# A two-block transformer kernel on one core: first projection in three passes, 22 modulation sums moved, sparse values in one run

## The chip, the core and the metric

The kernel is one program on one core of a Trainium2 chip. Its engines are TensorE (PE in the profile, its weight loads PEld), VectorE (DVE), ScalarE (ACT), GpSimd (POOL) and SyncE (SP). SP and POOL issue the transfers. The metric is the device time of one execution in microseconds (us), lower is better; it is given as the median of several runs.

## What is computed

The input is a sequence of 512 tokens of width 1024, in float32. The first block has a mixer (window attention and a gated delta rule, both fed by one input projection), cross attention to 256 memory rows, and a SwiGLU feed-forward layer. The second block has four more feed-forward layers, a dilated attention and a sparse attention (compressed, selected and sliding branch); its norms are modulated by vectors made from a condition `c`. The parts that matter here:

```python
# first block: the input projection (w_in: 1024 x 2832)
h = _rms_norm(x, g_mix_pre[l])
proj = h @ w_in[l]
aq, ak, av, dqkv, dgate, dalpha, dbeta = jnp.split(proj, IN_SPLITS, axis=-1)
...
# its feed-forward layer
f = _swiglu(_rms_norm(x, g_ffn_pre[l]), w_gate_up[l], w_down[l])
```

The modulation is `silu(c) @ w_ada`, 160 x 128 numbers. Each group of 128 is one "modulation sum": 128 rows of 1024 weights, multiplied by `silu(c)` and summed along the row.

## The kernel before

The program is written engine by engine (`pe_run`, `act_run`, `dve_run`, and blocks for POOL and SP), with semaphores between them. What stands in those functions is the order in which an engine works; there is no scheduler. All activations are held with channels on the partitions: `h` is 8 tiles of 128 channels x 512 tokens. `e.stage_end(name)` is a meeting point of PE, ACT and DVE.

**Weights.** SP streams 128 x 4096 slabs into two slab buffers, in the order of `STREAM`; a buffer is loaded again when its last reader says so (`slab_used`). SP's queue is, in this order: vec (203 KB), const (194 KB), x in four transfers, slabs 0 and 1, `c_row`, positions, tables, then the slabs one by one.

**Two kinds of product.** In `pe_slab` and `pe_token_major` (rows of L735, L756 and L774) a matmul takes float32 operands straight from the slab. The trace records each such matmul as two instructions. In `pe_parts` and its kin (L794, L799 and L800) the weight and the activation are split in two parts of type float32r: `w_hi` (a rounded copy, made by ACT, `act_w_hi`, L1039), `w_lo` (the rest, a subtraction on DVE, `dve_w_lo`, L1216), `x_hi` and `x_lo` in the same way. A product is then three matmuls, hi x hi, lo x hi and hi x lo, each one instruction. There are four buffers (`PARTS`) for split weights, one slab quarter each. TensorE frees one when it has left it, ACT fills its `w_hi`, DVE its `w_lo`, so that the weights are up to four tiles ahead.

**The first projection** (stage `w_in`) has 22 feature tiles of 8 products and a token-major part (4 groups of tokens, 144 columns). Around it, DVE convolves the 12 tiles of the delta rule (L2912 and four times L2914) from what ACT copies out of the banks.

**The modulation sums** (`dve_ada`, L1450) are 160 DVE instructions, each on a 128 x 1024 row block that POOL loads (L3169, 512 KB each). They are put beside other work in three turns of `ADA_TURNS = (42, 35, 83)`: turn 0 in the first projection with five buffers, turn 2 in the first feed-forward layer with three. POOL loads the next block into a buffer when the sum on it is done.

**The feed-forward layer** runs in two halves of 12 and 10 hidden tiles. Each half has an expansion (for a pair of tiles, gate and up: product and split of one hidden tile, L1367 and L1370) and a down projection of 8 tiles. `modulations` says how many sums go where.

**Sparse attention** has 32 units of two heads and 128 queries, with b+1 key blocks, b from 0 to 3. For each unit, DVE takes the maximum (L2428), ACT the exponentials (L2460), DVE scales them (L2451, semaphore `weighed`), TensorE turns the weights (L2411, 6 to 18 blocks of 128 x 128, up to four to one of two banks), ACT copies each bank (L2471), and TensorE multiplies them by the values (L2394, 6 to 18 matmuls). The stages of three units overlap. In iteration i TensorE does the scores of unit i+1 (L2366), values of unit i-2, turns of unit i-1, with the values cut in shares that stand between the groups of turns.

## Time and profile before

| | us |
|---|---|
| median of three runs | 3896.53 (3895.29 to 3897.41) |
| profiled execution, device time | 3898.42 |
| its span in the profile | 3896.6 |
| first projection, from first product to last | 22.25 to 185.83 |
| sparse attention | 3269.80 to 3474.00 |

The page gives PE 94% of the span busy, DVE 48%, ACT 36%. A group of rows names line, engine, operation, the tiles written and read, then busy time and the mean of one. In brackets stands how long the engine was idle before, and what ended the wait.

### The profile page before, as it was taken

The page shows a single profiled execution, that of the slowest core. Times are in us where ns is not written, and L with a number is a line of the kernel's source. Part 1 is how long each engine was busy: PE and PEld are TensorE (multiplying, and loading weights), DVE is VectorE, ACT ScalarE, POOL GpSimd, SP SyncE. Part 2 cuts the span into 40 slices and gives each one's busy share as a digit, 9 for nine tenths or more (in the row PEclk, how much of TensorE's full clock was granted, in tenths as well). Part 3 has the DMA queues.
Part 4 walks back from the last instruction along what each step waited for, and adds up shares of the span by engine and source line. Part 5 has one row for each costly group of instructions (what it writes and reads, how often), then busy time and mean ns, then how long its engine had stood idle before and what let it go on. Part 6 is the DMA issues. An engine that isn't in the chain of part 4 may idle for free.

```text
span 3896.6 us, 49558 instructions
## 1 busy us (share of the span) xinstructions
PE 3678.8 (94%) x19120; PEld 2903.7 (75%) x19120; DVE 1886.0 (48%) x3841; ACT 1395.4 (36%) x2478; POOL 107.3 (3%) x183
## 2 busy tenths in 40 slices
PE   8879999989998999999999989999899998889999
PEld 3458975778887888776767768888788886568887
DVE  4656735566566333454555544333433345654333
ACT  1142212432233222455555543223322233763222
POOL 1100000011111000000000000000000000000000
PEclk9979999989999999999999989999999999999999
DMA  6500015426662232211111212222222221002222
GB/s 253 194 1 1 1 60 194 154 92 229 216 226 110 77 117 76 78 69 50 49 50 49 71 53 90 96 97 96 88 81 103 81 73 44 1 28 82 89 106 76
DMA packets 47157, 360.79 MB, mean 93 GB/s; under 512 B 5216, under 2 KB 5600, under 8 KB 28128
## 3 DMA queue, kind: packets, MB, share of 16 engines
q1 hardware_dynamic: 23472, 270.36, 18.9%
q0 software_dynamic: 23472, 87.50, 6.4%
q8 instruction: 144, 2.36, 0.3%
q14 instruction: 69, 0.57, 0.0%
HBM read 355.74 MB, written 2.10 MB: 92 GB/s over the span
## 4 chain that ended last, share of the span: by engine, by line
PE 85%; DVE 8%; issue 4%; ACT 2%; DVEq 1%; DMA 0%; PEld 0%; ACTq 0%; PEldq 0%; POOL 0%; SPq 0%; POOLq 0%
PE bank L794 20%; PE bank L800 20%; PE bank L799 20%; PE bank L756 5%; PE bank L1597 5%; PE bank L2411 2%; PE bank L1931 1%; PE bank L1948 1%; PE bank L2394 1%; PE bank L1919 1%; PE bank L774 1%; PE bank L1907 1%; PE bank L735 1%; PE bank L723 1%; PE bank L1894 1%
## 5 line engine op out<-in xcount | busy, mean ns | idle before, releaser
L794 PE MATMUL bank<-x_hi_sb,w_hi_sb 128*128 128x512 f32 x2712 | 1085.4, 400 | 54.8 <-DVE w_lo_sb L1216 15.4
L800 PE MATMUL bank<-x_hi_sb,w_lo_sb 128*128 128x512 f32 x2712 | 1064.0, 392 | 0.9 <-issue 0.9
L799 PE MATMUL bank<-x_lo_sb,w_hi_sb 128*128 128x512 f32 x2712 | 1063.1, 392 | 0.0
L794 PEld LDWEIGHTS bank<-x_hi_sb,w_hi_sb 128*128 128x128 f32 x2712 | 512.9, 189 | 196.7 <-issue 67.5
L1039 ACT ACTIVATE w_hi_sb<-slab_sb 128x1024 fp32r<-128x1024 f32 (+2 forms) x525 | 475.8, 930 | 438.0 <-PE bank L794 254.5
L1216 DVE TENSOR_TENSOR w_lo_sb<-slab_sb,w_hi_sb 128x1024 fp32r<-128x1024 f32 (+2 forms) x525 | 544.7, 1070 | 166.7 <-ACT w_hi_sb L1039 150.4
L800 PEld LDWEIGHTS bank<-x_hi_sb,w_lo_sb 128*128 128x128 f32 x2712 | 512.5, 189 | 113.1 <-issue 2.3
L799 PEld LDWEIGHTS bank<-x_lo_sb,w_hi_sb 128*128 128x128 f32 x2712 | 513.5, 189 | 100.8
L1367 DVE TENSOR_TENSOR hid_sb<-silu_gate_sb,bank 128x512 f32<-128x512 f32 x110 | 75.6, 688 | 620.4 <-PE bank L800 620.4
L794 PE MATMUL bank<-hid_hi_sb,w_hi_sb 128*128 128x512 f32 x880 | 343.3, 390 | 0.0
L800 PE MATMUL bank<-hid_hi_sb,w_lo_sb 128*128 128x512 f32 x880 | 342.8, 390 | 0.0
L799 PE MATMUL bank<-hid_lo_sb,w_hi_sb 128*128 128x512 f32 x880 | 342.8, 390 | 0.0
L1123 ACT ACTIVATE hid_hi_sb<-hid_sb 128x512 f32 (+1 forms) x110 | 69.5, 632 | 588.7 <-DVE hid_sb L1367 588.7
L800 PEld LDWEIGHTS bank<-hid_hi_sb,w_lo_sb 128*128 128x128 f32 x880 | 165.4, 188 | 34.5
L799 PEld LDWEIGHTS bank<-hid_lo_sb,w_hi_sb 128*128 128x128 f32 x880 | 165.5, 188 | 34.2
L794 PEld LDWEIGHTS bank<-hid_hi_sb,w_hi_sb 128*128 128x128 f32 x880 | 165.5, 188 | 34.2
L3020 DVE SCALAR_TENSOR_TENSOR h_sb<-bank,fold_sb,h_sb 128x512 f32<-128x512 f32 x64 | 48.1, 751 | 293.3 <-PE bank L800 293.3
L1120 ACT ACTIVATE silu_gate_sb<-bank 128x512 f32<-128x512 f32 x110 | 65.7, 597 | 265.8 <-PE bank L800 265.8
L1597 PE MATMUL bank<-sq_sb 128*128 128x128 f32 x1088 | 134.7, 288 | 6.3 <-DVE sq_sb L1790 6.3
L1597 PEld LDWEIGHTS bank<-sq_sb 128*128 128x128 f32 x1088 | 131.9, 203 | 9.4 <-DVE sq_sb L1790 7.4
L756 PE MATMUL bank<-xn_sb,slab_sb 128*128 128x512 f32 x288 | 124.8, 593 | 1.3 <-issue 1.3
L1450 DVE CUSTOM_DVE_ANT_0 keep_sb<-keep_sb,tables_sb 128x1024 f32<-128x1024 f32 x104 | 122.8, 1221 | 3.9 <-DMA keep_sb<-ada 2.7
(356 smaller groups left out, 3971.5 us busy)
## 6 DMA issues: line engine op xcount, KB each, us to landing
slab_sb<-weights SPq DMA_DIRECT2D x80, 2048.0 KB, 7.8
slab_sb<-weights SPq DMA_DIRECT2D x44, 1536.0 KB, 6.5
keep_sb<-ada POOLq DMA_DIRECT2D x104, 512.0 KB, 4.9
slab_sb<-weights SPq DMA_DIRECT2D x20, 1280.0 KB, 6.0
work_sb<-ada POOLq DMA_DIRECT2D x49, 512.0 KB, 5.4
tables_sb<-ada POOLq DMA_DIRECT2D x7, 512.0 KB, 6.5
h_sb<-x SPq DMA_DIRECT2D x4, 512.0 KB, 7.1
out<-h_sb SPq DMA_DIRECT2D x8, 256.0 KB, 2.0
```

Of the source, the lines that this page charges most:

```text
L756: mm = pe.matmul(bank[s][:, 0:width], slab[i][:, k * stride + t * P:k * stride + t * P + cols], x(k), start=k == 0, stop=k == nkt - 1)
L794: mm = pe.matmul(out, w_hi[p][:, w], hi, start=first, stop=False)
L799: pe.matmul(out, w_hi[p][:, w], lo, start=False, stop=False)
L800: return pe.matmul(out, w_lo[p][:, w], hi, start=False, stop=last)
L1039: e.eng.activation(w_hi[p][:, 0:cols], e.raw[:, quarter * cols:(quarter + 1) * cols], ACT.Copy).then_inc(w_hi_ready, 1)
L1120: act.activation(sg[:, :], bank[s][:, :], ACT.Silu).then_inc(gate_ready, 1)
L1123: act.activation(hid_hi[:, at + pair, :], hid[:, pair, :], ACT.Copy).then_inc(hid_hi_ready, 1)
L1216: dve.tensor_tensor(w_lo[p][:, 0:cols], slab[e.raw_at][:, quarter * cols:(quarter + 1) * cols], w_hi[p][:, 0:cols].bitcast(F32), ALU.subtr ...
L1367: dve.tensor_tensor(hid[:, pair, :], sg[:, :], bank[s][:, :], ALU.mult).then_inc(product_ready, 1)
L1450: dve.tensor_tensor_reduce(out=buf, in0=buf, in1=c_row, scale=1.0, scalar=0.0, op0=ALU.mult, op1=ALU.add, accum_out=mod[:, n:n + 1]).then_ ...
L1597: mm = pe.matmul(b[:, x * P:(x + 1) * P], l(x), r(x), start=n == 0, stop=n == len(prods) - 1)
L2411: mm = eng.transpose(turn_bank[t][:, (x - at) * P:(x - at + 1) * P], n_p[(i - 1) % 3][:, x * P:(x + 1) * P], ident)
```

## The change

The slabs of `w_in` are laid out tile by tile, and the projection uses split weights and a split activation (`dve_scale_split`), all in three passes. The token-major part gets 256 columns instead of 144. ACT splits the first slab before it takes the root of the norm. Of the 42 modulation sums in the projection 20 remain, on three buffers instead of five, and POOL loads their rows only when slab 0 has landed. The other 22 go to the first feed-forward layer: three per tile in the down projection of half 0, four instead of three per hidden tile in the expansion of half 1. In sparse attention all values of a unit stand in one run ahead of the wait for `weighed` and the turns. Places of buffers in `work` move with it.

```diff
-ADA_TURNS = (42, 35, 83)
+ADA_TURNS = (20, 35, 105)
...
+    ends = np.concatenate([*slabs_of(w_in[:, 20 * P:22 * P], P), *slabs_of(w_in[:, 22 * P:], 2 * P)], 1)
+    w_in = np.concatenate([slabs_by_tile(w_in[:, :20 * P]), ends[None]], 0)
...
-        ada_loaded = [[sem(f"ada_loaded{t}_{i}") for i in range(n)] for t, n in enumerate((5, 5, 3))]
-        ada_used = [[sem(f"ada_used{t}_{i}") for i in range(n)] for t, n in enumerate((5, 5, 3))]
+        ada_loaded = [[sem(f"ada_loaded{t}_{i}") for i in range(n)] for t, n in enumerate((3, 5, 3))]
+        ada_used = [[sem(f"ada_used{t}_{i}") for i in range(n)] for t, n in enumerate((3, 5, 3))]
...
-        b1_qkv = cut(work, 0, 12, S)
-        b1_vtm = cut(work, 6144, NB, 144)
-        b1_cv = [cut(work, 6720, S + 4), cut(work, 6720 + 516, S + 4)]
+        b1_qk = cut(work, 14336, 6, S)
+        b1_qkv = cut(work, 4096, 12, S)
+        b1_vtm = cut(work, 10240, NB, 144)
+        b1_cv = [cut(work, 10816, S + 4), cut(work, 10816 + 516, S + 4)]
         b1_gate = cut(keep, 0, 4, S)
-        b1_tmp = cut(work, 7760, 4, S)
+        b1_tmp = cut(work, 11848, 4, S)
         b1_cos, b1_sin = b1_tmp[:, 0, :], b1_tmp[:, 1, :]
 
-        P_SB = [cut(work, 9856 + 768 * i, 768) for i in range(3)]
-        PT = [cut(work, 12160 + 768 * i, 768) for i in range(2)]
+        P_SB = [cut(work, 11848 + 768 * i, 768) for i in range(3)]
+        PT = [cut(work, 14152 + 768 * i, 768) for i in range(2)]
...
+        def dve_scale_split(e, gain):
+
+            dve = e.eng
+            s = e.take(e.S, e.sc)
+            for i in range(KT + 2):
+                if i < KT:
+                    dve.scalar_tensor_tensor(out=y[:, i, :], in0=h[:, i, :], scalar=gain[:, i:i + 1],
+                                             in1=e.S.bank[s][:, :], op0=ALU.mult, op1=ALU.mult).then_inc(normed, 1)
+                if i >= 2:
+                    k = i - 2
+                    dve.wait_ge(x_hi_ready, e.nth(x_hi_ready))
+                    dve.tensor_tensor(x_lo[:, k, :], y[:, k, :], x_hi[:, k, :].bitcast(F32),
+                                      ALU.subtract).then_inc(x_lo_ready, 1)
+            dve.drain().then_inc(e.S.free[s], 1)
+
...
-        ada_bufs = [[cut(work, 9856 + D * i, D) for i in range(5)],
+        ada_bufs = [[cut(keep, 2048, D), cut(tables, 2688, D), cut(work, 11848, D)],
...
-                    groups = (blocks(units[i - 1][1]) + 3) // 4 if 1 <= i <= n else 0
-
-                    def values(share, shares):
-                        if i < 2:
-                            return
+                    if i >= 2:
                         tile, b = units[i - 2]
-                        kv, total = tile // 4, 1 + 2 * (b + 1)
-                        if share == 0:
-                            if i - 2 in opens:
-                                outs[tile] = e.give(e.A, e.acc)
-                            eng.wait_ge(copied, e.nth(copied))
-                        mm = None
-                        for x in range(total * share // shares, total * (share + 1) // shares):
+                        kv = tile // 4
+                        if i - 2 in opens:
+                            outs[tile] = e.give(e.A, e.acc)
+                        eng.wait_ge(copied, e.nth(copied))
+                        for x in range(1 + 2 * (b + 1)):
                             for hh in heads:
                                 br, k = (0, 0) if x == 0 else (1 + (x - 1) // (b + 1), (x - 1) % (b + 1))
                                 at = at_of(b, br, hh) + k * P
                                 v = n_vcmp[:, 64 * kv:64 * kv + 64] if br == 0 else \
                                     n_v[:, k, 128 * (br - 1) + 64 * kv:128 * (br - 1) + 64 * kv + 64]
                                 mm = eng.matmul(e.A.bank[outs[tile]][64 * hh:64 * hh + 64, b * P:(b + 1) * P], v,
-                                                n_pt[par][:, at:at + P], start=x == 0, stop=x == total - 1)
-                        if share == shares - 1:
-                            mm.then_inc(pv_done, 1)
-                            if i - 2 in closes:
-                                eng.drain().then_inc(e.A.full[outs[tile]], 1)
-
-                    shares = max(groups - 1, 1)
-                    values(0, shares)
+                                                n_pt[par][:, at:at + P], start=x == 0, stop=x == 2 * (b + 1))
+                        mm.then_inc(pv_done, 1)
+                        if i - 2 in closes:
+                            eng.drain().then_inc(e.A.full[outs[tile]], 1)
                     if 1 <= i <= n:
                         eng.wait_ge(weighed, e.nth(weighed))
                         total = blocks(units[i - 1][1])
                         for at in range(0, total, 4):
-                            if 2 <= at // 4 <= shares:
-                                values(at // 4 - 1, shares)
                             t = e.give(tp, e.tp)
                             for x in range(at, min(at + 4, total)):
                                 mm = eng.transpose(turn_bank[t][:, (x - at) * P:(x - at + 1) * P],
...
-            pe_slab_opening(e, xn, normed)
+            pe_parts_opening(e, x_hi, x_lo)
             for _ in range(4):
-                pe_slab(e, range(4), KT, 512, lambda k: xn[:, k, :])
-            pe_slab(e, range(2), KT, 512, lambda k: xn[:, k, :],
-                    more=[lambda sl: pe_token_major(e, sl, xn, KT, 256, 512, 144)])
+                pe_parts(e, PARTS, KT, x_hi, x_lo, by_tile=True)
+            e.slab.next()
+            for _ in range(2):
+                pe_tile_parts(e)
+            pe_token_parts(e, 2, 2 * P, 2 * P)
+            pe_settle(e)
+            e.seat(normed).pos += KT
...
+            for q in range(PARTS):
+                act_w_hi(e, q, D)
             act_sums_root(e, False)
+            for k in range(KT):
+                act.wait_ge(normed, e.nth(normed))
+                act.activation(x_hi[:, k, :], y[:, k, :], ACT.Copy).then_inc(x_hi_ready, 1)
             act.wait_ge(tables_first, 48)
             act.activation(c_row, c_row, ACT.Silu).then_inc(c_ready, 1)
             for t in range(22):
+                if t < 20:
+                    act_w_hi(e, t % PARTS, D)
                 if t < 4:
-                    act_copy(e, sq[:, t, :], scale=0.125)
+                    act_copy(e, b1_qk[:, t, :], scale=0.125)
                 elif t < 6:
-                    act_copy(e, sq[:, t, :])
+                    act_copy(e, b1_qk[:, t, :])
...
+            for q in range(PARTS):
+                dve_w_lo(e, q, D)
             dve_sums_done(e)
             e.sc.pos += 1
-            dve_scale(e, h, V("g_mix_pre"), xn, normed)
-            dve.wait_ge(c_ready, 1)
-            dve_ada(e, 14)
+            dve_scale_split(e, V("g_mix_pre"))
+            for t in range(6):
+                dve_w_lo(e, t % PARTS, D)
+                if t == 0:
+                    dve.wait_ge(c_ready, 1)
+                dve_ada(e, 2)
             e.acc.pos += 22
             for t in range(12):
+                dve_w_lo(e, (t + 6) % PARTS, D)
...
-                dve_ada(e, 1)
-            dve_ada(e, 16)
+            for q in (2, 3):
+                dve_w_lo(e, q, D)
+            dve_ada(e, 8)
...
                 if at in ("first", "mid", "last"):
-                    dve_ada(e, 3)
+                    dve_ada(e, 4 if half else 3)
                 elif half == 0 or at < 5:
-                    dve_ada(e, 2 if half == 0 and at < 4 else 1)
+                    dve_ada(e, 1 if half else 3)
...
-            eng.wait_ge(vec_loaded, 32)
+            eng.wait_ge(slab_loaded[0], 16)
```

`slabs_by_tile` is the layout that the feed-forward weights have already; in the expansion loop of `dve_ffn`, `modulations` is called once per hidden tile.

On DVE, at the start of the program, these are the rows before (L1229 adds squares, L1310 is the reciprocal of the RMS, L1317 scales the tiles, L1450 is a modulation sum in two instructions):

```order
L2892 MEMSET work_sb 128x2
L1229 TENSOR_TENSOR work_sb<-work_sb 128x512 x6
L1310 RECIPROCAL small_sb<-small_sb 128x4
L1317 SCALAR_TENSOR_TENSOR xn_sb<-h_sb,vec_sb,bank 128x512 x8
L1450 ISA work_sb,mod_sb<-work_sb,tables_sb 128x1024
L1450 ISA mod_sb 128x1
```

And these are they after (L1219 is now `w_lo`, L1313 the reciprocal, L1330 the scaling and L1335 `x_lo`):

```order
L1232 TENSOR_TENSOR work_sb<-work_sb 128x512 x6
L1219 TENSOR_TENSOR w_lo_sb<-slab_sb,w_hi_sb 128x1024 x4
L1313 RECIPROCAL small_sb<-small_sb 128x4
L1330 SCALAR_TENSOR_TENSOR y_sb<-h_sb,vec_sb,bank 128x512 x3
L1335 TENSOR_TENSOR x_lo_sb<-y_sb,x_hi_sb 128x512
L1330 SCALAR_TENSOR_TENSOR y_sb<-h_sb,vec_sb,bank 128x512
```

Four `w_lo` now stand ahead of the reciprocal, and three scalings ahead of the first `x_lo`.

On DVE, at the convolution tiles of the projection, before (L2912 and L2914 are one tile):

```order
L1450 ISA work_sb,mod_sb<-work_sb,tables_sb 128x1024
L1450 ISA mod_sb 128x1
L2912 TENSOR_SCALAR work_sb<-work_sb,vec_sb 128x512
L2914 SCALAR_TENSOR_TENSOR work_sb<-work_sb,vec_sb 128x512 x4
L1450 ISA work_sb,mod_sb<-work_sb,tables_sb 128x1024
```

and after (L1468 is the modulation sum, L2935 and L2937 are one tile):

```order
L1468 ISA work_sb,mod_sb<-work_sb,tables_sb 128x1024
L1468 ISA mod_sb 128x1
L1219 TENSOR_TENSOR w_lo_sb<-slab_sb,w_hi_sb 128x1024
L2935 TENSOR_SCALAR work_sb<-work_sb,vec_sb 128x512
L2937 SCALAR_TENSOR_TENSOR work_sb<-work_sb,vec_sb 128x512 x4
L1219 TENSOR_TENSOR w_lo_sb<-slab_sb,w_hi_sb 128x1024
```

The sum behind each convolution tile is gone, and a `w_lo` stands ahead of each.

On TensorE, in sparse attention, one iteration before (scores of the next unit, values of a unit with b = 1, turns of a unit with b = 2, the 31-column scores):

```order
L2366 MATMUL bank<-keep_sb,work_sb 128x256 x4
L2394 MATMUL bank<-work_sb,keep_sb 64x128 x2
L2411 MATMUL bank<-const_sb,work_sb 128x128 x8
L2394 MATMUL bank<-work_sb,keep_sb 64x128 x4
L2411 MATMUL bank<-const_sb,work_sb 128x128 x4
L2394 MATMUL bank<-work_sb,keep_sb 64x128 x4
L2411 MATMUL bank<-const_sb,work_sb 128x128 x2
L2366 MATMUL bank<-keep_sb,work_sb 128x31 x2
```

and the same iteration after, with the start of the next (L2384 scores, L2406 values, L2417 turns):

```order
L2384 MATMUL bank<-keep_sb,work_sb 128x256 x4
L2406 MATMUL bank<-work_sb,keep_sb 64x128 x10
L2417 MATMUL bank<-const_sb,work_sb 128x128 x14
L2384 MATMUL bank<-keep_sb,work_sb 128x31 x2
L2384 MATMUL bank<-keep_sb,work_sb 128x512 x4
```

Eight of the ten value matmuls have moved ahead of the first turn, where TensorE waits for `weighed`, and the fourteen turns follow each other.

## Rows read from the trace of the kernel before

**Rows 1.** The page: the chain that ended last, by engine
```profile
PE 85%; DVE 8%; issue 4%; ACT 2%; DVEq 1%; DMA 0%; PEld 0%; ACTq 0%; PEldq 0%; POOL 0%; SPq 0%; POOLq 0%
```

**Rows 2.** Windows: stretch, length, busy PE, PEld, DVE, ACT, POOL, clock, DMA, GB/s
```profile
22.25:185.83 163.58, 162.24 (x416) 75.12 (x416) 97.03 (x154) 14.21 (x23) 19.53 (x37) 1.00 0.55 206
...
3269.80:3474.00 204.20, 169.47 (x1536) 113.59 (x1536) 134.33 (x709) 153.72 (x507) 0.00 (x0) 0.95 0.01 1
```

**Rows 3.** Timelines of DVE and POOL, landings of L3169: first layer, half 1
```profile
1060.21 0.69 DVE L1367 TENSOR_TENSOR hid_sb<-silu_gate_sb,bank 128x512 f32<-128x512 f32 x1 [3.00 <-PE bank L800]
...
1062.31 1.22 DVE L1450 CUSTOM_DVE_ANT_0 keep_sb<-keep_sb,tables_sb 128x1024 f32<-128x1024 f32 x1
...
1065.75 2.36 DVE L1216 TENSOR_TENSOR w_lo_sb<-slab_sb,w_hi_sb 128x1024 fp32r<-128x1024 f32 x2
1071.09 0.69 DVE L1367 TENSOR_TENSOR hid_sb<-silu_gate_sb,bank 128x512 f32<-128x512 f32 x1 [2.98 <-PE bank L800]
...
1063.83 0.53 POOL L3169 DMA_DIRECT2D keep_sb<-ada  x1 [8.07 <-DVE mod_sb L1450]
...
DMA to landing us min/median/max: 3.3/4.8/5.4
```

**Rows 4.** Timeline of PE: one slab of the first projection
```profile
80.10 27.70 PE L756 MATMUL bank<-xn_sb,slab_sb 128*128 128x512 f32 x64 [0.26 <-issue]
```

**Rows 5.** Line L873: third pass of a token-major part, durations and starts
```profile
L873 PE MATMUL bank<-w_lo_sb,x_hi_sb x32: 277/283/415, 2770.3 to 2783.0; 128*128 128x256 f32 x32
```

**Rows 6.** Timeline of PE: second and third matmul of the first layer
```profile
835.28 0.63 PE L799 MATMUL bank<-x_lo_sb,w_hi_sb 128*128 128x512 f32 x1
835.71 0.63 PE L800 MATMUL bank<-x_hi_sb,w_lo_sb 128*128 128x512 f32 x1
```

**Rows 7.** Timeline of DVE and PE: start of the projection
```profile
19.01 0.18 DVE L1310 RECIPROCAL small_sb<-small_sb 128x4 f32<-128x4 f32 x1 [4.03 <-ACT small_sb L992]
...
21.35 5.36 DVE L1317 SCALAR_TENSOR_TENSOR xn_sb<-h_sb,vec_sb,bank 128x512 f32<-128x512 f32 x8 [2.17 <-PE bank L966]
...
22.25 29.62 PE L735 MATMUL bank<-xn_sb,slab_sb 128*128 128x512 f32 x64 [0.93 <-DVE xn_sb L1317]
```

**Rows 8.** DMA, 0 to 40 us (GB/s: slices of 1 us), and landings of L3218
```profile
GB/s 0 29 286 190 266 356 311 320 422 418 397 406 467 397 434 426 434 426 438 406 426 422 418 377 414 391 425 422 475 376 409 108 0 0 0 0 66 311 295 262
...
slab_sb<-weights SPq DMA_DIRECT2D x2, 2048.0 KB, 18.9
h_sb<-x SPq DMA_DIRECT2D x4, 512.0 KB, 7.1
...
3.56 1.25 SPq L3218 DMA_DIRECT2D slab_sb<-weights  x2
...
DMA to landing us min/median/max: 16.1/18.9/21.7
```

**Rows 9.** Timelines of DVE and ACT: a convolution tile, two w_hi
```profile
101.60 0.49 DVE L2912 TENSOR_SCALAR work_sb<-work_sb,vec_sb 128x512 f32<-128x512 f32 x1 [2.08 <-ACT work_sb L2715]
...
105.16 1.22 DVE L1450 CUSTOM_DVE_ANT_0 work_sb<-work_sb,tables_sb 128x1024 f32<-128x1024 f32 x1
...
1061.58 1.99 ACT L1039 ACTIVATE w_hi_sb<-slab_sb 128x1024 fp32r<-128x1024 f32 x2
```

**Rows 10.** Timeline: one iteration of sparse attention (L2366 is the next scores)
```profile
3394.75 1.09 PE L2411 MATMUL bank<-const_sb,work_sb 128*128 128x128 f32 x8 [1.33 <-DVE work_sb L2451]
...
3395.52 1.07 ACT L2471 ACTIVATE sq_sb<-bank 128x512 f32<-128x512 f32 x2
3395.78 0.66 PE L2394 MATMUL bank<-work_sb,keep_sb 128*64 128x128 f32 x8
3396.36 0.66 PE L2411 MATMUL bank<-const_sb,work_sb 128*128 128x128 f32 x4
...
3397.91 2.21 PE L2366 MATMUL bank<-keep_sb,work_sb 64*128 64x31 f32 x12
```

**Rows 11.** Waits in sparse attention: who waited for whom, us, times, longest
```profile
PE bank L2411 <- DVE work_sb L2451: 18.3, 16, 3.7
```

12 lines of the change are left out of this document (6 added, 6 removed).

## Prediction

> **What bounds the kernel now.** I began with the page. TensorE is on the chain that ended last for 85% of the span, DVE for 8% [rows 1]. So a stage gets shorter if TensorE has less to do there, or if a wait in front of it goes. The change touches three stages, and I read each by its stretch, then by its timeline. In the first projection TensorE is busy 162.24 us of 163.58 while DVE has 97.03 of work [rows 2]: TensorE bound, others with room. In sparse attention it is busy 169.47 of 204.20 us, with ACT at 153.72 and DVE at 134.33 [rows 2]; there the three engines wait for each other. In the first feed-forward layer I read the timeline instead: DVE does its work for a pair of tiles and then waits 2.98 us for TensorE [rows 3], so TensorE sets the pace and DVE has that much room.
>
> **Projection, TensorE's work.** A product is one 128x128 weight tile times 512 tokens. As float32 it is recorded as two instructions, and a slab of 32 products takes 27.70 us, 0.865 us each [rows 4]. The same product in three passes of the split form stands in the feed-forward layer: one pair of tiles, 16 products, from 1060.21 to 1071.09, is 10.88 us, so 0.680 us [rows 3]. Before the change the stage has 22 tiles of 8 products plus the token-major part. After it, 176 x 0.680 = 119.7 us. The token-major part becomes 96 matmuls of 256 columns. The same shape runs elsewhere, with 32 triplets whose starts span 12.7 us over 31 steps [rows 5], so 13.1 us. After an idle stretch the first matmuls come every 0.43 us [rows 6] instead of 0.227 (10.88 / 48), the lower clock of 1.2 GHz against 2.4. Nine of them cost 1.8 us more. With 0.6 us for drains the stage is 135.2 us of TensorE time where it was 163.58: 28.4 saved.
>
> **Projection, its start.** Before, the first product starts at 22.25, right after the first scaled tile [rows 7]. Now it needs the slab split too, and the order shows the four w_lo subtractions ahead of the reciprocal of the RMS. So the start is: slab 0 landed, w_hi of the first quarter on ACT (about 1.05 us), four w_lo on DVE, then reciprocal, spread, three scales, one x_lo. Slab 0 lands at 3.6 + 16.1 = 19.7 us now [rows 8]. Ahead of it in its queue are vec and const (0.4 MB) and x (four times 512 KB); with its own 2048 KB that is 4.6 MB [rows 8]. The 1 us slices of moved bytes add up to 4.6 MB at 14.8 us [rows 8], and the five modulation rows that share those slices now will wait for slab 0. Bounds: 14.8 if nothing else is moved and the last byte counts, 19.7 as before. I take 16.0. Then 16.0 + 1.05 + 4 x 1.15 (two w_lo take 2.36, [rows 3]) = 21.7. From reciprocal to first scale it is 2.34 us, from 19.01 to 21.35 [rows 7]. Three scales at 0.67 (5.36 for eight, [rows 7]) and one subtraction of 512 columns, about 0.7, give 26.7. That is 4.5 us later than 22.25 (3.3 to 8.2 by the bounds).
> From 10 to 30 us the slices show 377 to 475 GB/s [rows 8]. The Trainium skill (DMA: Bandwidth & Descriptors, Where 436 GB/s comes from) says that for HBM to SBUF the HBM side binds, near 358 GB/s. By that rate, as an estimate, slab 0 would land about 1 us later than I take; the trace of this core, alone on its memory, is above it, so the trace decides.
>
> **Projection, do ACT and DVE keep up?** A tile is 8 x 0.680 = 5.44 us of TensorE. A convolution tile costs DVE 3.56 us (101.60 to 105.16, [rows 9]); with a w_lo of 1.15 that is 4.7, and the sum of 1.15 that stood there is gone, or it would be 5.9. The first six tiles carry w_lo and two sums: 3.5 us. ACT has a w_hi (two take 1.99, [rows 9]) and a copy of 512 columns. Weights are made four tiles ahead, so a late one is absorbed. At the end the last w_lo can be done about 21 us before TensorE is (two gate tiles and the token-major part follow it), and eight sums over three buffers need some 15 (three rounds of 1.15 + 0.4 + 3.6). All this is hidden; if w_hi, w_lo, copy and convolution stood in series instead, some 6.3 us per tile, twelve tiles would give back 10 us. Net of the stage: 28.4 - 4.5 = **23.9 us saved**.
>
> **The 22 sums in the feed-forward layer.** In half 0 the down projection goes from two or one to three sums per tile; a tile lasts 12 x 0.680 = 8.16 us there, and DVE then has three sums (3.4), two w_lo of 768 columns (about 1.8) and one copy (under 1). Hidden. In half 1 each pair gets a fourth sum, but there are three buffers. Now a group starts at 1062.31; the first sum's buffer is asked for again at 1063.83, and a row lands 3.3 to 5.4 us after its issue, median 4.8 [rows 3]. The first of a group has the queue to itself, so I take 3.6 for it. The fourth sum then starts not 3.44 but about 5.2 us after the group's start (4.9 to 6.4 by the minimum and the median), ends at 6.3, and two w_lo end at 8.6. DVE's next product is due 8.78 after the group's start (1071.09), and 2.98 of them are idle now [rows 3]. So 2.9 us are added to a slack of 2.98. What is late next is the w_lo: its first is needed by TensorE at the end of the running pair, 1.3 us after it is made. Beside slab loads the group runs up to 0.9 us over. Over ten pairs I take **1.0 us lost**, bounds 0 and 9 (0.9 each). If the cover were gone, each sum would cost 1.15 us, 11.5 for the ten.
>
> **Sparse attention.** Each unit of TensorE is: scores ahead, values of the unit before the last, a wait for DVE's weights, then turns in groups of four through two banks. Now most of the values stand between the turns. Counted over a round of 16 units, 88 of 192 value matmuls stand behind the wait, in two rounds 176. Four, recorded as eight, take 0.58 us (3395.78 to 3396.36, [rows 10]), so 0.117 x 176 = 20.5 us move ahead of the wait. TensorE waits there for weights in two of their three buffers alone 18.3 us in 16 waits, 1.14 us each [rows 11]; 12 units of 16 have something to move, 0.86 us on average. The cover is uneven, since a heavy unit meets a short wait; I take three quarters, 15.5 us. Then the turns have nothing between them and meet ACT. In the unit at 3394.75, eight turns are out after 1.03 us, but ACT starts copying them only at 3395.52, 0.54 us each [rows 10]. The third group can start at 3395.52 + 0.54 + 0.06 = 3396.12, 0.35 after the first eight, and the block ends at 2.33 us instead of 3.16 (3397.91, [rows 10]). The wait in front, 1.33, takes the moved 0.93 us. So this unit gains 0.83. The copy's pace costs 0.35 to 0.45 in each of the 24 units, some 8.5 in all. Net **7.0 us saved**; the ends are 0 (turns fully paced by ACT, or the loop over DVE and ACT as long as now) and 15.5 (no pacing).
>
> **The sum.** 23.9 - 1.0 + 7.0 = 29.9. The profiled execution took 3898.42 us with a span of 3896.6; its own time would be 3868.5. It lies 1.9 us above the median of the three runs, 3896.53, against which I set the forecast: 3866.6.
>
> **The rivals.**
> *A, the turns are ACT's.* ACT is busy 153.72 of 204.20 us [rows 2] and every copy stands behind its exponentials. If the loop exponentials, copies, turns, scores sets the unit, the run of values brings nothing: 3873.6. Against it: in the unit I followed ACT idles between copies. Chance 0.12.
> *B, DVE becomes the pace of half 1.* For it: 0.1 us of slack left per pair, and a median landing of 4.8 us [rows 3]. With 0.9 per pair: 3874.6. Chance 0.10.
> *C, a late start.* Slab 0 lands as before, or the w_hi are paced otherwise: 3.7 us more, 3870. Chance 0.08.
> *D, DVE paces the projection's convolution tiles*, 6.3 us a tile: 10 given back, 3876.6. Against: four tiles of lead. Chance 0.05. Should it wait for the last sums at the stage's end as well, another 15 us is lost and the time is within 0.2% of now; 0.02.
> *E, slower.* One mechanism: in half 1 the fourth sum holds the w_lo so long that TensorE idles each pair and falls to the lower clock, where a matmul takes 0.43 instead of 0.227 us [rows 6]. 48 matmuls a pair are then 9.7 us longer, ten pairs 97: 3963. It decides from 3.9 us lost per pair on (39 in all, against the 31 of the other two terms); the fourth sum would have to start 9 us after the group's start, where the longest landing here gives 7.0. Chance 0.03.
> My forecast, with small shifts of its terms, has the remaining 0.60.
>
> **How the numbers follow.** The low end is the projection with slab 0 at 14.8 (1.2 more), no loss in the layer, and sparse attention near 14.4: 3857. The high end takes in A, B, C and D alone and A with B: 3882. Outside lie some 15 in 100. This kernel's measurement tells about 0.2%, 7.8 us, from no change. Faster by more: 0.95; within: 0.02; slower: 0.03.
>
> **What would show it.** In the changed profile: first three-pass product near 26.7; 5.44 us per tile, no wait for w_lo after the first four; last token-major matmul near 162; slab 0 landed near 16; in half 1 a wait of DVE for the modulation row of 1 to 2.5 us before each fourth sum, pairs still 10.88 to 11.1; in the sparse stage the wait for DVE down from 18.3 to under 9 us, a new wait of turns for ACT of some 9. Wrong would be: tiles of over 5.6 us, TensorE's wait for w_lo in half 1 above a microsecond a pair, or a sparse stage still above 200 us.

## Result, and the profile after

The changed kernel takes 3867.02 us (median, 3863.18 to 3869.01) against 3896.54: ratio 0.9925, 95% interval 0.9912 to 0.9938, 29.5 us less. The forecast was 3866.6. It was right in the sum and wrong in two of its three terms, which cancelled:

| | forecast, us | in the profile | the edit by itself on the chip |
|---|---|---|---|
| projection | 23.9 saved | 24.7 saved | 22.1 saved (beside a fourth row buffer; by the interval of the ratio 14 to 25) |
| 22 sums in the feed-forward layer | 1.0 lost | 12.1 lost | 12.3 lost |
| sparse attention | 7.0 saved | 16.9 saved | 16.3 saved |
| together | 29.9 | 29.5 | |

The profiled execution is the fastest of its four (3863.18, span 3861.4); its span is 35.2 under the one of before. That the three terms read from the profiles add up to the same 29.5 as the two medians is chance. The 5.7 us beyond the three terms lie in stages that the change does not touch, 4.5 of them between the first down tile of the second feed-forward layer and sparse attention. In the profiles of this study, with the same code there, that stretch varied from 1896 to 1906 us.

The page of the changed kernel, the chain by engine and two groups:

```profile
PE 83%; DVE 8%; issue 4%; ACT 3%; DVEq 1%; DMA 1%; PEld 0%; ACTq 0%; PEldq 0%; POOL 0%; SPq 0%; POOLq 0%
...
L797 PE MATMUL bank<-x_hi_sb,w_hi_sb 128*128 128x512 f32 x2888 | 1156.7, 401 | 61.6 <-DVE w_lo_sb L1219 19.3
...
L1468 DVE CUSTOM_DVE_ANT_0 keep_sb<-keep_sb,tables_sb 128x1024 f32<-128x1024 f32 x133 | 157.9, 1220 | 44.6 <-DMA keep_sb<-ada 42.7
```

TensorE is still the chain (before 85%, [rows 1]). What is new is in the other rows: TensorE waits more for `w_lo`, and DVE 42.7 us for modulation rows, where before it was 2.7.

**The projection.** The start, a timeline of all engines, and the landing of the first two slabs:

```profile
16.17 3.90 ACT L1042 ACTIVATE w_hi_sb<-slab_sb 128x1024 fp32r<-128x1024 f32 x4 [3.56 <-DMA slab_sb<-weights]
...
17.25 4.63 DVE L1219 TENSOR_TENSOR w_lo_sb<-slab_sb,w_hi_sb 128x1024 fp32r<-128x1024 f32 x4 [4.53 <-ACT w_hi_sb L1042]
...
22.02 0.18 DVE L1313 RECIPROCAL small_sb<-small_sb 128x4 f32<-128x4 f32 x1
...
24.37 2.06 DVE L1330 SCALAR_TENSOR_TENSOR y_sb<-h_sb,vec_sb,bank 128x512 f32<-128x512 f32 x3 [2.17 <-PE bank L969]
...
27.18 0.77 PE L797 MATMUL bank<-x_hi_sb,w_hi_sb 128*128 128x512 f32 x1 [2.85 <-DVE x_lo_sb L1335]
```

```profile
DMA to landing us min/median/max: 12.6/14.7/16.9
```

The slab lands at 3.56 + 12.6 = 16.2 and DVE splits from 17.25 on; then reciprocal, spread, scales, and the first product at 27.18, 4.9 later than [rows 7]. The windows of three stretches (columns as in [rows 2]): the projection, the expansion of half 1, sparse attention. Below them, from the timeline, the first matmul of the next stage, which started at 197.10 before:

```profile
27.18:160.98 133.80, 132.91 (x624) 111.66 (x624) 95.87 (x135) 37.98 (x49) 8.96 (x17) 1.00 0.45 165
1022.46:1128.86 106.40, 101.44 (x433) 83.00 (x432) 73.91 (x109) 27.52 (x36) 19.01 (x36) 0.97 0.73 253
3252.20:3439.84 187.64, 158.52 (x1536) 112.38 (x1537) 134.12 (x709) 152.36 (x507) 0.00 (x0) 0.97 0.01 2
```

```profile
172.41 7.63 PE L791 MATMUL bank<-work_sb,const_sb 128*128 128x512 f32 x12 [11.27 <-ACTq L497]
```

The projection is 133.8 us at a granted clock of 1.00 where it was 163.58 [rows 2]; only its first seven matmuls came every 0.43 us, although that row gives them the same clock. In the waits of this stretch TensorE has none for `w_lo`. DVE waited 17.0 us for rows, and TensorE did not wait for it.

**Half 1 of the feed-forward layer.** Its ten products take 106.40 us from first to last; nine steps of 10.88 would be 97.9. From the last down tile of half 0 (1011.58) to the last of half 1 it is 180.7 us, before 168.6. Waits of 1000 to 1195, and the fourth sum of a usual group, of a late one and of the last one (timeline of DVE):

```profile
DVE keep_sb L1468 <- DMA keep_sb<-ada: 23.5, 11, 5.3
...
PE bank L797 <- DVE w_lo_sb L1219: 7.5, 3, 3.3
```

```profile
1029.68 1.22 DVE L1468 CUSTOM_DVE_ANT_0 keep_sb<-keep_sb,tables_sb 128x1024 f32<-128x1024 f32 x1 [1.62 <-DMA keep_sb<-ada]
...
1079.75 1.23 DVE L1468 CUSTOM_DVE_ANT_0 keep_sb<-keep_sb,tables_sb 128x1024 f32<-128x1024 f32 x1 [5.33 <-DMA keep_sb<-ada]
...
1136.06 1.23 DVE L1468 CUSTOM_DVE_ANT_0 keep_sb<-keep_sb,tables_sb 128x1024 f32<-128x1024 f32 x1 [1.69 <-DMA keep_sb<-ada]
```

The landing of the row that each of two groups waited for, by its issue:

```profile
L3193 POOL DMA_DIRECT2D keep_sb<-ada x1: 528/528/528, 1037.0 to 1037.0; - x1
...
DMA to landing us min/median/max: 3.5/3.5/3.5
```

```profile
L3193 POOL DMA_DIRECT2D keep_sb<-ada x1: 527/527/527, 1072.4 to 1072.4; - x1
...
DMA to landing us min/median/max: 7.3/7.3/7.3
```

And what SP had issued ahead of the second, and what TensorE did then (timelines):

```profile
1068.68 0.34 SPq L3232 DMA_DIRECT2D slab_sb<-weights  x1
```

```profile
1082.17 0.80 PE L797 MATMUL bank<-x_hi_sb,w_hi_sb 128*128 128x512 f32 x1 [3.33 <-DVE w_lo_sb L1219]
1082.77 0.63 PE L802 MATMUL bank<-x_lo_sb,w_hi_sb 128*128 128x512 f32 x1
1083.19 0.63 PE L803 MATMUL bank<-x_hi_sb,w_lo_sb 128*128 128x512 f32 x1
...
1138.18 0.47 PE L797 MATMUL bank<-hid_hi_sb,w_hi_sb 128*128 128x512 f32 x1 [2.56 <-DVE w_lo_sb L1219]
```

In a usual group the first buffer's row lands after 3.5 us and the fourth sum waits 1.6: what the forecast said, and the pair keeps its 10.88. Eight of the ten groups are like this, with landings of 3.5 to 3.7 us. The two others asked for the row 3.6 and 3.8 us after SP had issued a 2 MB slab load. There the row needs 6.4 or 7.3 us, the `w_lo` is late, and TensorE stands for 1.6 and 3.3 us. (A row asked for 6.9 us after such a load landed in 3.6 us, so it depends on how far the load is.) The third wait, 2.6 us, is another case. Its row landed in the usual 3.7 us, but it is the last group, and the `w_lo` behind its fourth sum is the one that the down projection needs.

After the gap of 3.33 a matmul comes every 0.43 us instead of 0.227: the granted clock of 1082.17 to 1087.90 is 0.50, 1.2 GHz against 2.4. Fourteen matmuls then take 2.9 us too long. Behind the third wait the granted clock of 1139.40 to 1144.00 is 0.63, and nine matmuls take 1.6 us too long. Behind the first, of 1.64 us, it stays 1.00. 7.5 us of waits and 4.5 us of lower clock are 12.0 of the 12.1. The Trainium skill (DMA: Bandwidth & Descriptors, Queues, rings and completion order) says that a DMA engine goes round robin between the queues it has work for; by that rule a row on POOL's queue shares each engine with a slab on SP's, and the trace agrees, with 3.5 against 6.4 and 7.3 us.

**Sparse attention.** It is 187.6 us long where it was 204.5. TensorE's waits ahead of turns, and one iteration, the one of [rows 10]:

```profile
PE bank L2417 <- DVE work_sb L2457: 8.0, 10, 2.6
...
PE bank L2417 <- ACT sq_sb L2477: 5.3, 14, 1.0
PE bank L2417 <- ACT work_sb L2477: 5.0, 16, 0.6
...
PE bank L2417 <- DVE xn_sb L2457: 2.8, 3, 1.0
```

```profile
3365.80 1.31 PE L2406 MATMUL bank<-work_sb,keep_sb 128*64 128x128 f32 x20
3367.57 1.09 PE L2417 MATMUL bank<-const_sb,work_sb 128*128 128x128 f32 x8 [0.46 <-DVE work_sb L2457]
3368.97 0.93 PE L2417 MATMUL bank<-const_sb,work_sb 128*128 128x128 f32 x6 [0.31 <-ACT sq_sb L2477]
3369.83 2.21 PE L2384 MATMUL bank<-keep_sb,work_sb 64*128 64x31 f32 x12
```

Waits for DVE are down to 10.8 us (with the third buffer 24.3 before), waits for ACT in front of turns up from nothing to 10.3, each new group 0.31 in this unit: near the forecast. The waits in front of turns that the profile puts down to "issue" went from 5.8 to 0.8 us besides. This unit takes 2.26 us from first turn to next scores, where the forecast said 2.33.

The forecast had left out two things. One is in the run lengths. A run is a row of matmuls of one kind with none of the other between them: 8 turns take 1.03 us and 4 take 0.59 [rows 10], which is 0.11 each and 0.15 for the run. Going through the shares of all units, 96 such runs are gone. The other is the clock. Below are windows of the kernel before and of that of experiment 4 (`thin_shares`): the whole stage of each, then a stretch at the lower clock of each (in these, only TensorE's busy time, clock and DMA):

```profile
3269.85:3474.34 204.49, 169.47 (x1536) 113.56 (x1536) 134.33 (x709) 153.96 (x507) 0.00 (x0) 0.95 0.01 1
...
3253.40:3455.86 202.46, 172.01 (x1537) 115.47 (x1537) 134.16 (x709) 154.18 (x507) 0.00 (x0) 0.93 0.01 1
...
3381.50:3384.50 3.00, 3.00 (x17) 0.50 0.02 5
...
3407.50:3414.00 6.50, 6.38 (x34) 0.50 0.00 0
```

(The row of the changed kernel is the third of the windows above.) TensorE's idle time in the stage went from 35.0 to 29.1 us and its busy time from 169.5 to 158.5, together the 16.9. Counted in windows of 0.5 us, TensorE was busy for 17 us of the stage at a granted clock of 0.50 before and for 7 us after. At half speed that is 8.6 and 3.7 us lost, so 4.9 of the 11.0 us of busy time are the clock. In the profiles of this study the loss is 7.3 to 8.7 us with the order of before and 2.2 to 6.9 with the new one. So it goes with the order, but it varies, and it is not the price of the runs.

### The profile page after: what moved, and what is told of

It reads as the page before. It is cut to its first block, busy times and chain, and to the rows that moved or that the text cites. A ratio compares the mean times of both kernels' runs of the same rounds, so it can differ in the third digit from the quotient of the medians.

```text
span 3861.4 us, 50061 instructions
## 1 busy us (share of the span) xinstructions
PE 3639.3 (94%) x19328; PEld 2940.1 (76%) x19328; DVE 1916.9 (50%) x3873; ACT 1421.8 (37%) x2510; POOL 107.3 (3%) x183
## 4 chain that ended last, share of the span: by engine, by line
PE 83%; DVE 8%; issue 4%; ACT 3%; DVEq 1%; DMA 1%; PEld 0%; ACTq 0%; PEldq 0%; POOL 0%; SPq 0%; POOLq 0%
PE bank L797 21%; PE bank L802 21%; PE bank L803 21%; PE bank L1615 5%; PE bank L759 2%; PE bank L1949 1%; PE bank L1937 1%; PE bank L1966 1%; PE bank L2417 1%; DVE w_lo_sb L1219 1%; PE bank L2384 1%; PE bank L1925 1%; PE bank L777 1%; PE bank L726 1%; PE bank L2406 1%
## 5 line engine op out<-in xcount | busy, mean ns | idle before, releaser
L797 PE MATMUL bank<-x_hi_sb,w_hi_sb 128*128 128x512 f32 x2888 | 1156.7, 401 | 61.6 <-DVE w_lo_sb L1219 19.3
L803 PE MATMUL bank<-x_hi_sb,w_lo_sb 128*128 128x512 f32 x2888 | 1134.0, 393 | 0.0
L802 PE MATMUL bank<-x_lo_sb,w_hi_sb 128*128 128x512 f32 x2888 | 1133.9, 393 | 0.0
L797 PEld LDWEIGHTS bank<-x_hi_sb,w_hi_sb 128*128 128x128 f32 x2888 | 547.4, 190 | 211.9 <-issue 71.2
L1042 ACT ACTIVATE w_hi_sb<-slab_sb 128x1024 fp32r<-128x1024 f32 (+2 forms) x549 | 500.9, 936 | 508.3 <-PE bank L797 319.6
L1219 DVE TENSOR_TENSOR w_lo_sb<-slab_sb,w_hi_sb 128x1024 fp32r<-128x1024 f32 (+2 forms) x549 | 573.4, 1076 | 185.2 <-ACT w_hi_sb L1042 168.7
L803 PEld LDWEIGHTS bank<-x_hi_sb,w_lo_sb 128*128 128x128 f32 x2888 | 546.9, 189 | 117.7
L802 PEld LDWEIGHTS bank<-x_lo_sb,w_hi_sb 128*128 128x128 f32 x2888 | 548.1, 190 | 107.8
L1468 DVE CUSTOM_DVE_ANT_0 keep_sb<-keep_sb,tables_sb 128x1024 f32<-128x1024 f32 x133 | 157.9, 1220 | 44.6 <-DMA keep_sb<-ada 42.7
L1388 DVE TENSOR_TENSOR hid_lo_sb<-hid_sb,hid_hi_sb 128x512 f32 (+1 forms) x110 | 76.1, 692 | 93.8 <-ACT hid_hi_sb L1126 93.8
```

The lines of the kernel that those rows point to most:

```text
L797: mm = pe.matmul(out, w_hi[p][:, w], hi, start=first, stop=False)
L802: pe.matmul(out, w_hi[p][:, w], lo, start=False, stop=False)
L803: return pe.matmul(out, w_lo[p][:, w], hi, start=False, stop=last)
L1042: e.eng.activation(w_hi[p][:, 0:cols], e.raw[:, quarter * cols:(quarter + 1) * cols], ACT.Copy).then_inc(w_hi_ready, 1)
L1219: dve.tensor_tensor(w_lo[p][:, 0:cols], slab[e.raw_at][:, quarter * cols:(quarter + 1) * cols], w_hi[p][:, 0:cols].bitcast(F32), ALU.subtr ...
L1388: dve.tensor_tensor(hid_lo[:, at + pair, :], hid[:, pair, :], hid_hi[:, at + pair, :].bitcast(F32), ALU.subtract).then_inc(hid_lo_ready, 1)
```

## Experiments

Each was timed beside the kernel before, which gave 3895.4 to 3897.6. The changed kernel gave 3867.02 at first and 3864.78 in experiment 9, so a difference to it is uncertain by some 2 us.

**1. Sparse attention alone.** The kernel before with the block of the change on sparse attention, nothing else.

> The kernel before with only the sparse values in one run. The changed kernel's sparse stage took 187.6 us where it took 204.5, 16.9 less. Theory T1 (the gain belongs to this edit: 13.5 us less waiting for DVE, 96 fewer changes between value and turn matmuls at about 0.15 us each, less some 10 us of new waits for ACT): 3896.5 - 17 = 3879.5, range 3876 to 3883. Rival R1, the prediction's 7.0 (the rest came from the run or from elsewhere): 3889.5. Rival R2, nothing: 3896.5.

3879.2 us, ratio 0.9959 (0.9945 to 0.9972): 16.3 saved, and the stage is 187.1 us long. The gain belongs to this edit; the prediction's 7.0 is too small by more than half. What T1 gives as its parts this run does not separate.

**2. The 22 sums alone**, on the kernel before.

```diff
-ADA_TURNS = (42, 35, 83)
+ADA_TURNS = (20, 35, 105)
...
-            dve_ada(e, 14)
+            dve_ada(e, 12)
...
-                dve_ada(e, 1)
-            dve_ada(e, 16)
+            dve_ada(e, 8)
...
-                    dve_ada(e, 3)
+                    dve_ada(e, 4 if half else 3)
                 elif half == 0 or at < 5:
-                    dve_ada(e, 2 if half == 0 and at < 4 else 1)
+                    dve_ada(e, 1 if half else 3)
```

> The kernel before with only the 22 modulation sums moved to the first feed-forward layer; the projection stays in float32 with five row buffers. Theory T2 (the fourth row of a group in half 1 lands too late beside the slab loads, TensorE waits for w_lo three times and runs at the lower clock after it): 12 to 14 us slower, 3909.5. Where the slab loads fall against the groups may shift with the projection, so 6 to 16. Rival R3, the prediction's 1.0: 3897.5. Rival R4 (in the projection DVE's 42 sums had cost TensorE something, which comes back): below 3896.5.

3907.77 us, ratio 1.0032 (1.0020 to 1.0045): 12.3 lost, 11.8 of it between the last down tiles of the two halves. The waits of half 1 are there without the new projection:

```profile
DVE keep_sb L1450 <- DMA keep_sb<-ada: 24.4, 11, 5.2
...
PE bank L794 <- DVE w_lo_sb L1216: 7.2, 3, 3.1
```

**3. A fourth row buffer in half 1.** The changed kernel; the buffer takes the place of hidden tiles 10 and 11, which half 1 has not.

```diff
-                    [cut(keep, D * i, D) for i in range(3)]]
+                    [*(cut(keep, D * i, D) for i in range(3)), cut(work, 9216, D)]]
...
                 if n < pieces:
+                    if turn == 2:
+                        if n < 60:
+                            i, use = n % 3, n // 3
+                        else:
+                            i = (n - 60) % 4
+                            use = (n - 60) // 4 + (20 if i < 3 else 0)
+                        return ada_bufs[2][i], ada_loaded[2][i], ada_used[2][i], use
```

> The changed kernel with a fourth row buffer for the sums of half 1 (in the place of two hidden tiles that half 1 does not use); the same sums at the same places. Theory T2 (it is the reload of the first buffer, not DVE's own work): all four rows of a group are asked for a pair ahead, the pairs are back at 10.88 us, 11 to 13 us gained: 3867 - 12 = 3855. Rival R5 (DVE's four sums and two w_lo alone are too long, or the DMA engines cannot carry four rows a pair beside the slabs): no more than 3 us gained, 3864.

3853.15 us, ratio 0.9892 (0.9877 to 0.9907), 13.9 under the changed kernel (11.6 under its second median). TensorE's waits for `w_lo` in this stretch, and a group on DVE with its four sums in a row:

```profile
PE bank L797 <- DVE w_lo_sb L1219: 0.8, 1, 0.8
```

```profile
1057.27 0.69 DVE L1385 TENSOR_TENSOR hid_sb<-silu_gate_sb,bank 128x512 f32<-128x512 f32 x1 [1.84 <-PE bank L803]
...
1062.80 1.22 DVE L1475 CUSTOM_DVE_ANT_0 work_sb<-work_sb,tables_sb 128x1024 f32<-128x1024 f32 x1
...
1068.15 0.69 DVE L1385 TENSOR_TENSOR hid_sb<-silu_gate_sb,bank 128x512 f32<-128x512 f32 x1 [1.85 <-PE bank L803]
```

Same sums, same places, same bytes; only the reload is no longer waited for. The pairs are back at 10.88, and DVE has 1.85 us left in each. From the last down tile of half 0 to that of half 1 it is 170.6 us, against 180.7 and, before the change, 168.6. So 10.1 of the 12.1 us were the wait for the row and what came of it. The other 2.0 stay with four sums per group, 0.8 of them as the wait above, at the down projection. R5 falls for the most part: neither DVE's own work nor the DMA engines' total was too much within the pairs.

**4. One pair of values between the turns.** The changed kernel in sparse attention with the shares of before, but so cut:

```diff
-                        for x in range(total * share // shares, total * (share + 1) // shares):
+                        lead = total - shares + 1
+                        for x in (range(lead) if share == 0 else range(lead + share - 1, lead + share)):
```

> The changed kernel, but in sparse attention each share behind the first keeps one pair of value matmuls between the groups of turns (48 of them, 96 changes of kind more than in the changed kernel); all other values stay ahead of the wait. Theory T1 (a change costs about 0.15 us, so 96 are 14.4, and what they fill is about 10 us of waits for ACT): slower than the changed kernel by 2 to 7 us, 3871. The prediction's own account (no price for a change, the turns' wait for ACT 8.5 us, filled by 48 pairs of 0.22 us): faster by 4 to 8 us, 3861.

3879.77 us, ratio 0.9957 (0.9943 to 0.9971), 12.8 over the changed kernel (15.0 over its second median). The prediction's account has the wrong sign. T1 has the right one, but I had the size too small. Waits, and a piece of one iteration:

```profile
PE bank L2430 <- DVE work_sb L2470: 13.9, 13, 3.7
...
PE bank L2430 <- DVE xn_sb L2470: 3.8, 4, 2.0
...
PE bank L2430 <- ACT sq_sb L2490: 1.2, 2, 0.6
```

```profile
3376.90 0.44 PE L2413 MATMUL bank<-work_sb,keep_sb 128*64 128x128 f32 x4
3377.28 0.66 PE L2430 MATMUL bank<-const_sb,work_sb 128*128 128x128 f32 x4
3377.87 0.44 PE L2413 MATMUL bank<-work_sb,keep_sb 128*64 128x128 f32 x4
```

The waits of turns for ACT are gone but for 1.6 us, as both said. Four turns take 0.59 us (3377.28 to 3377.87), four recorded values 0.38. The stage is 14.8 us longer than the changed kernel's, by the windows above: 13.5 more busy for the same matmuls and 1.3 more idle. In the idle time, 8.7 us less for ACT met 6.9 more for DVE and 5.0 more under "issue". In the busy time, 8.1 us are the lower clock (24 us busy at 0.50 instead of 7, half of it lost), which neither theory had; only this one profile shows this order. The 5.4 left are less than 96 x 0.15 = 14.4. A sum of waits cannot settle this, since the end of a run in front of a wait is counted as busy (eight turns as 1.09 us, 1.03 without a wait behind them). So the 0.15 us per change is shown in single rows, and its share of the stage's gain is not.

Against the kernel before, the stage is only 2.0 us shorter. There 80 of the 176 value matmuls have moved ahead of the wait, and the number of runs is the same. So moving values brought little here as long as the runs stayed; 3.2 us more of lower clock than before are in that figure.

**5. Is it the tile shape?** The kernel before, its values with 128 columns. It leaves out attention's right values, and only its times count.

```diff
-                                v = n_vcmp[:, 64 * kv:64 * kv + 64] if br == 0 else \
-                                    n_v[:, k, 128 * (br - 1) + 64 * kv:128 * (br - 1) + 64 * kv + 64]
-                                mm = eng.matmul(e.A.bank[outs[tile]][64 * hh:64 * hh + 64, b * P:(b + 1) * P], v,
-                                                n_pt[par][:, at:at + P], start=x == 0, stop=x == total - 1)
+                                v = n_vcmp[:, 0:P] if br == 0 else n_v[:, k, 128 * (br - 1):128 * br]
+                                mm = eng.matmul(e.A.bank[outs[tile]][:, b * P:(b + 1) * P], v,
+                                                n_pt[par][:, at:at + P], start=x == 0 and hh == 0,
+                                                stop=x == total - 1 and hh == 1)
```

> The kernel before, sparse values in shares, but each value matmul takes 128 value columns instead of 64 and writes the whole bank, so that both heads add up in one place (the values are no longer attention's; the number, order, rows and waits of the matmuls are the same). A value matmul is then a 128*128 tile as a turn is, and not 128*64. In the trace a run of n recorded matmuls of either kind takes 0.15 us + n x 0.055 (values) or n x 0.11 (turns): 4 values 0.37, 2 turns 0.37. Theory T3 (the 0.15 us is the price of going from one tile shape of TensorE to another): runs of 4 values between turns take 0.22 instead of 0.37, 128 changes between values and turns cost nothing, up to 19 us less TensorE time, of which waits take some back: 3884, range 3878 to 3889. Rival T4 (the 0.15 us is a price of every change of operands or banks, whatever the shape): 3896.5, runs of 4 still 0.37.

3918.03 us, ratio 1.0050 (1.0038 to 1.0062), 22.6 slower: neither theory's time. The timeline says why, and still decides between them:

```profile
3407.94 1.06 PE L2393 MATMUL bank<-work_sb,keep_sb 128*128 128x128 f32 x8
3408.84 0.60 PE L2411 MATMUL bank<-const_sb,work_sb 128*128 128x128 f32 x4
3409.27 1.06 PE L2393 MATMUL bank<-work_sb,keep_sb 128*128 128x128 f32 x8
```

Four turns between two runs of values now take 0.43 us (3408.84 to 3409.27) where they took 0.59: the 0.15 is gone once both kinds have one tile shape. T3 holds for these runs, T4 falls. But eight recorded value matmuls take 0.90 instead of 0.58, 0.11 each instead of 0.055. Over 768 that is some 44 us. The two heads' matmuls go to the two 64-column halves in turn. They may have run side by side, or a matmul of 64 columns may take half the time by itself; all of them in this kernel alternate between the halves, so no run here tells the two apart. The Trainium skill (TensorEngine Tiling (Array Packing), Key Properties) says that a change of tiling mode drains the engine, and that tiles work independently. The trace fits both, at 0.15 us for a change of shape.

**6. Rows asked for early.** The changed kernel with one line as it was:

```diff
-            eng.wait_ge(slab_loaded[0], 16)
+            eng.wait_ge(vec_loaded, 32)
             load_ada(0)
```

> The changed kernel, but POOL asks for the first three modulation rows when vec has landed, as in the kernel before, and not when slab 0 has. The step of the prediction: slab 0 landed at 19.7 with five rows beside it and at 16.2 with none; three rows are 1.5 MB, at some 420 GB/s 3.7 us. So slab 0 near 19, the first product near 30 instead of 27.18, the time 3869.5 (2 to 3.5 us over the changed kernel's 3867.0). Rival: the rows only take bandwidth that the slab does not need: first product within 1 us of 27.2.

3865.93 us, ratio 0.9917 (0.9903 to 0.9930). In the profile slab 0 lands at 3.6 + 17.6 = 21.2, and the first product is at

```profile
32.22 0.76 PE L797 MATMUL bank<-x_hi_sb,w_hi_sb 128*128 128x512 f32 x1 [2.85 <-DVE x_lo_sb L1335]
```

5.0 later, more than the 3.7 that I had from the bytes. In the kernel before, five rows asked for just as early left slab 0 at 19.7 [rows 8], 3.5 later than 16.2. So the delay is real, but its size does not follow from the number of rows. The next stage starts 5.4 later too, and the first down tile of the second feed-forward layer still 5.6; by the end of the profile 2.4 are left. The median is 1.1 below the changed kernel's (1.1 above its second one), and the intervals of the two ratios allow some -10 to +4 us. So the late start is shown by the profile, and that it costs its 5 us at the end is not: whether they are won back behind the layer or lost in the scatter of the stages there stays open.

**7. Root and reciprocal ahead of the split weights.** The changed kernel; in DVE's order `dve_sums_done(e)` goes ahead of the four `dve_w_lo` in the same way.

```diff
+            act_sums_root(e, False)
             for q in range(PARTS):
                 act_w_hi(e, q, D)
-            act_sums_root(e, False)
```

> The changed kernel with two orders swapped at the start: ACT takes the root of the norm ahead of the four w_hi, DVE the reciprocal ahead of the four w_lo. The reciprocal then falls in DVE's idle time before slab 0 (near 17 instead of 22.02) and its 2.34 us of spreading lie under the w_lo. First product near 24.8 instead of 27.18, 2.4 us gained: 3864.6. If instead something else holds the start (the slab, or x_hi), less than 1 us.

3862.41 us (3855.47 to 3865.95), ratio 0.9906 (0.9892 to 0.9919); first product at 26.33, 0.85 earlier instead of 2.4. The median is 2.4 under the changed kernel's second one, but its own runs lie 10 apart, so what the start brings can't be read from it. ACT's timeline shows what is late now, the root that the `w_hi` wait for:

```profile
17.21 0.26 ACT L995 ACTIVATE small_sb<-bank,small_sb 128x4 f32<-128x4 f32 x1 [3.85 <-PE bank L959]
17.65 3.90 ACT L1042 ACTIVATE w_hi_sb<-slab_sb 128x1024 fp32r<-128x1024 f32 x4 [0.17 <-issue]
```

**8. Root and reciprocal behind the first split weight, with the fourth buffer.**

```diff
-            for q in range(PARTS):
-                act_w_hi(e, q, D)
+            act_w_hi(e, 0, D)
             act_sums_root(e, False)
+            for q in range(1, PARTS):
+                act_w_hi(e, q, D)
...
-            for q in range(PARTS):
-                dve_w_lo(e, q, D)
+            dve_w_lo(e, 0, D)
             dve_sums_done(e)
             e.sc.pos += 1
+            for q in range(1, PARTS):
+                dve_w_lo(e, q, D)
```

> The changed kernel with the fourth row buffer and, at the start, ACT: first w_hi, root, three w_hi; DVE: first w_lo, reciprocal, three w_lo. With the root ahead of all w_hi the first w_hi waited for it until 17.65 although slab 0 was there a microsecond earlier, and the first product came at 26.33 and 26.61. Now the root waits behind one w_hi and ends near 17.7, the reciprocal stands behind the first w_lo, near 18.6, its spreading ends near 21, under the other w_lo. First product 25.2 (against 27.2 to 27.6 in the changed order), 2 us gained: 3851.2. If the reciprocal comes too late for that, 26.3 as with the root first.

3852.18 us, ratio 0.9889 (0.9874 to 0.9904); timeline of the start:

```profile
22.48 2.07 DVE L1330 SCALAR_TENSOR_TENSOR y_sb<-h_sb,vec_sb,bank 128x512 f32<-128x512 f32 x3 [0.15 <-issue]
...
25.29 0.77 PE L797 MATMUL bank<-x_hi_sb,w_hi_sb 128*128 128x512 f32 x1 [4.35 <-DVE x_lo_sb L1335]
```

First product at 25.29, as expected, 1.9 us earlier. That is the fastest kernel of the study, 43.4 us under the kernel before and 12.6 under the changed kernel's second median. The fourth buffer has nearly all of it (3853.15 without the start); 1.9 us are too little to see in the median.

**9. Combinations and a control.** The edits of 3 and 7 together:

> The changed kernel with the fourth row buffer and with root and reciprocal first. Both are at different places and should add up: 3853.2 - 2.4 = 3850.8. If the earlier start shifts slab loads against the row groups of half 1, up to 2 us either way.

3853.47 us, ratio 0.9883 (0.9868 to 0.9898), first product at 26.61: the start's part is too small to see beside 3853.15.

Eleven sums moved on from half 1 instead of a fourth buffer, on the changed kernel:

```diff
-ADA_TURNS = (20, 35, 105)
+ADA_TURNS = (20, 46, 94)
...
-            dve_ada(e, 8)
+            dve_ada(e, 14)
             dve_sums_done(e)
...
-            dve_linear_parts(e, y, 2, lambda k: dve_ada(e, 3 if k < 3 else 2))
+            dve_linear_parts(e, y, 2, lambda k: dve_ada(e, 3))
...
-                    dve_ada(e, 4 if half else 3)
-                elif half == 0 or at < 5:
+                    dve_ada(e, 3)
+                elif half == 0 or at < 4:
```

> The changed kernel with 11 of the modulation sums moved on from half 1 of the first feed-forward layer: six to DVE's idle time of 13 us before the cross attention, five to its query projection. Half 1 is back at three sums per pair and four buffers are not needed. Theory T2: as the fourth buffer, 11 to 13 us gained, 3855; should the sums of the query projection come late for their w_lo, up to 3 us are given back. Rival R5 (four sums and two w_lo of DVE as such were not the cause, the later rows of turn 1 delay TensorE elsewhere): 3862 or more.

3856.82, ratio 0.9888 (0.9873 to 0.9903). Half 1 has no wait for `w_lo`, and from last down tile to last down tile it is 168.7 us, as before the change, which confirms T2 by another way. Some of it is lost again ahead of it, where the sums went: from the first matmul behind the projection to the first down tile it is 787.2 us, in the changed kernel 782.1 (in the other profiles up to 784.9).

The projection alone, as the kernel of experiment 3 with the sparse attention of before:

> The kernel with the fourth row buffer (3853.15 us) and the sparse attention of before, values in shares: what the projection in three passes brings when the two other parts are taken out. Theory: the parts add up, 3853.2 + 16.3 (what one run of values gave alone) = 3869.5, that is 27 us under the kernel before, the 24.7 by which the last product of the stage is earlier, and 1 to 3 in other stages. Rival: the parts help each other and the sum of the single ones is off by more than 5 us.

3873.4 (3868.94 to 3879.83), ratio 0.9949 (0.9936 to 0.9963): 22.1 saved, 4 less than the sum of the parts says and within its scatter; the next stage starts at 172.91, 0.5 later than in the changed kernel.

And the changed kernel once more:

> The changed kernel once more, unaltered, beside the two others of this call, as a measure of how far its median moves: 3867.0, within 2 us. Its profile should again show three waits of TensorE for w_lo in half 1, if they come from the phase of the slab loads and not from chance: the stage then loses 12 to 14 us again.

3864.78, ratio 0.9923 (0.9910 to 0.9937), with TensorE's three waits for `w_lo` in half 1 again (7.9 us). They are no chance of one run.

## Why the prediction was right, and where it was not

**Projection.** Right step by step. TensorE's part is 133.8 (135.2 forecast), a product 0.680, seven slow matmuls instead of nine. The token-major part took 11.6 us where the forecast had 13.1. The 0.6 us for drains in the sum is in no run. Slab 0 landed at 16.2 (16.0), the first product came at 27.18 (26.7), the last token-major matmul at 160.87 (162). ACT and DVE kept up, so rival D did not happen. Rival C neither, though experiment 6 shows that its cause, rows ahead of the slab, is real.

**Sums.** The mechanism was right and the size was not. The step that failed is "The first of a group has the queue to itself, so I take 3.6 for it". It had POOL's queue to itself, not the DMA engines: in two groups of ten, early in a slab load, the landing is 6.4 and 7.3. Besides, the forecast counted pairs only, and the last group's `w_lo` is for the down projection, where TensorE stood 2.6 us at a landing of 3.7. The clock behind the waits, 4.5 us, was priced in rival E alone. The bound of 9 took only the 5.4 of the kernel before, where three sums on three buffers never asked for the row at once. The range of the term was 0 to 9; it measured 12. Rival B named the wait and "0.9 per pair"; in truth seven groups of ten lose nothing and three lose 2 to 6 us, in part as lower clock. Rival E's chain (late `w_lo`, idle TensorE, lower clock) happened in small: for six and for three microseconds, not for the stage.

**Sparse attention.** Cover and pacing were near: 13.5 us less waiting for DVE, 18.5 with the waits under "issue" (15.5 forecast), 10.3 of waits of turns for ACT (8.5). The step that failed is the price of what moved, "0.117 x 176 = 20.5 us": it counts the matmuls and not the runs. The row that it cites gives 0.58 / 4 = 0.145 per matmul, with the run in it; where 0.117 comes from the prediction does not show. Each share between the turns also cost two changes of tile shape, 0.15 us each by single rows. And the sum has no term for the clock in this stage, which gave 4.9 of the 16.9 us between these two profiles. How the rest is shared between runs and waits stays open (experiment 4). The one unit that I followed was forecast to 0.07 us because its run lengths were read whole; the sum over the stage was made from a single price per matmul.

The total came out by luck: the sums cost 11 us more than forecast, and sparse attention saved 10 us more. The range held it; the argument for it held only in the first term.
